# Two transformer blocks in one kernel: other buffers for two weight blocks, another order of slabs and steps

## The reference

```python
z = rmsnorm(x) @ w_in_2                       # qa ka va | qb kb vb | ga gb
qa, ka = rope(qa), rope(ka)                   # 4 heads of 2 components
ya = diff_attention(qa, ka, va, lam)          # softmax 0 minus lam * softmax 1, then a norm per head
yb = chunk_band_attention(qb, kb, vb, bias)   # 8 heads, relative bias, chunk mask
x = x + (sigmoid(ga) * (ya @ w_up_a) + sigmoid(gb) * (yb @ w_up_b)) @ w_out_2
x = x + cross_attention(rmsnorm(x), rmsnorm(mem), w_cq, w_ckv, w_co)
x = x + swiglu(rmsnorm(x))
return rmsnorm(x)
```

## Time and profile before

| | |
|---|---|
| median of 3 runs | 970.59 us (970.41 to 971.19) |
| the profiled execution | 972.24 us, span 970.3 us |
| TensorE (PE) busy | 924.0 us, 95% of the span, 4289 products |
| VectorE (DVE) busy | 629.2 us, 65% |
| ScalarE (ACT) busy | 458.1 us, 47% |
| GpSimd (POOL) busy | 30.6 us, 3% |
| DMA | 178.11 MB, 184 GB/s on average, above 330 GB/s in the first four of 40 slices |

### The profile page before, as it was taken

How to read it: one execution, slowest core, us unless ns; L and a number is a source line. 1 busy time by engine, 2 the same in 40 slices (tenths; PEclk the granted TensorE clock), 3 DMA queues, 4 the chain that set the end, 5 groups by cost and what they waited for, 6 DMA issues and landing times.

```text
span 970.3 us, 12075 instructions
## 1 busy us (share of the span) xinstructions
PE 924.0 (95%) x4289; PEld 741.7 (76%) x4289; DVE 629.2 (65%) x1016; ACT 458.1 (47%) x707; POOL 30.6 (3%) x42
## 2 busy tenths in 40 slices
PE   3989999999999999999999999999999999999997
PEld 3877655678788888887888777788788788888785
DVE  4887999988755555676766454578655555555544
ACT  0544422465544444544645443574545455555432
POOL 2110000010000000000000000000000000000000
PEclk9999999999999999999999999999999999999999
DMA  9999322766475665575655333245461465555531
GB/s 332 349 366 331 125 86 88 259 223 207 141 260 176 191 194 174 216 261 174 197 194 174 130 115 103 87 174 193 135 214 44 131 205 185 173 187 198 178 130 44
DMA packets 103031, 178.11 MB, mean 184 GB/s; under 512 B 6318, under 2 KB 52635, under 8 KB 102986
## 3 DMA queue, kind: packets, MB, share of 16 engines
q1 hardware_dynamic: 96138, 151.23, 47.4%
q0 software_dynamic: 6848, 26.28, 7.3%
HBM read 176.39 MB, written 1.05 MB: 183 GB/s over the span
## 4 chain that ended last, share of the span: by engine, by line
PE 73%; DVE 9%; issue 7%; ACT 2%; DMA 1%; POOL 0%; DVEq 0%; POOLq 0%; ACTq 0%
PE bank L553 18%; PE bank L555 18%; PE bank L554 18%; PE bank L959 10%; DVE conv_out L1883 4%; DVE w_lo L1664 1%; ACT w_hi L1208 1%; PE bank L938 1%; PE bank L632 1%; PE bank L784 1%; DMA ada_raw<-in_w_ada 1%; PE bank L1153 1%; PE bank L1169 1%; PE bank L800 1%; PE bank L1103 1%
## 5 line engine op out<-in xcount | busy, mean ns | idle before, releaser
L1664 DVE TENSOR_TENSOR w_lo<-raw_weights,w_hi 128x1024 fp32r<-128x1024 f32 x267 | 324.7, 1223 | 238.4 <-ACT w_hi L1208 236.9
L1208 ACT ACTIVATE w_hi<-raw_weights 128x1024 fp32r<-128x1024 f32 x267 | 281.1, 1058 | 304.8 <-PE bank L555 227.5
L553 PE MATMUL bank<-w_hi,a_hi 128*128 128x512 f32 x808 | 322.8, 399 | 5.9 <-DVE w_lo L1664 3.3
L555 PE MATMUL bank<-w_hi,a_lo 128*128 128x512 f32 x808 | 316.1, 391 | 0.0
L554 PE MATMUL bank<-w_lo,a_hi 128*128 128x512 f32 x808 | 315.6, 391 | 0.0
L553 PEld LDWEIGHTS bank<-w_hi,a_hi 128*128 128x128 f32 x808 | 152.2, 188 | 43.3 <-issue 7.3
L555 PEld LDWEIGHTS bank<-w_hi,a_lo 128*128 128x128 f32 x808 | 152.1, 188 | 32.4
L554 PEld LDWEIGHTS bank<-w_lo,a_hi 128*128 128x128 f32 x808 | 152.3, 188 | 29.8 <-issue 0.2
L959 PE MATMUL bank<-w_hi,ff_hi 128*128 128x512 f32 x176 | 55.2, 395 | 0.8 <-DVE hidden_rows L2161 0.5
L959 PE MATMUL bank<-w_hi,ff_lo 128*128 128x512 f32 x176 | 54.3, 389 | 0.0
L959 PE MATMUL bank<-w_lo,ff_hi 128*128 128x512 f32 x176 | 54.3, 390 | 0.0
(11 more groups left out here) (265 smaller groups left out, 870.4 us busy)
## 6 DMA issues: line engine op xcount, KB each, us to landing
raw_weights<-in_w_in SPq DMA_DIRECT2D x40, 1024.0 KB, 5.2
raw_weights<-in_w_ffn_in SPq DMA_DIRECT2D x44, 512.0 KB, 4.6
raw_weights<-in_w_gate_up SPq DMA_DIRECT2D x44, 512.0 KB, 4.6
ada_raw<-in_w_ada POOLq DMA_DIRECT2D x10, 1024.0 KB, 8.7
ada_start<-in_w_ada POOLq DMA_DIRECT2D x10, 1024.0 KB, 12.9
raw_weights<-in_w_ffn_out SPq DMA_DIRECT2D x9, 1024.0 KB, 5.0
raw_weights<-in_w_down SPq DMA_DIRECT2D x9, 1024.0 KB, 4.9
raw_weights<-in_w_out SPq DMA_DIRECT2D x8, 1024.0 KB, 5.2
```

Of the source, the lines that this page charges most:

```text
L553: pe.matmul(ps, hi[:, kt, ts], wh, start=start, stop=False)
L555: return pe.matmul(ps, lo[:, kt, ts], wh, start=False, stop=stop)
L1208: act.activation(w_hi[:, slot, 0:m], raw[:, b % RAW, half * PIECE:half * PIECE + m], ACT.Copy)\
L1664: dve.tensor_tensor(w_lo[:, slot, 0:m], raw[:, b % RAW, half * PIECE:half * PIECE + m], w_hi[:, slot, 0:m], ALU.subtract).then_inc(lo_read ...
```

## The change

- Ada block 10 gets the buffer `ada_start[4]` and waits for the first product of slab 4 only; block 11 gets a new buffer `ada_tail` over rows that were used up, and waits for the first four products.
- The second modulation columns come after one top-8 round instead of three. The second native gate piece comes ahead of the first step of the first attention instead of inside it.
- Second block: five plain slabs qb, kb, qa, ka, vb; va, the second memory keys, four gate slabs and half of the memory values are mixed. Rope works on 8 heads at a time. qb and kb are transposed in the third slab, qa in the fifth, ka in steps 1 and 2 of the banded attention; the second memory keys' transposes go behind the first query slab of the cross attention.
- Differential steps: a mixed piece at each step, ahead of its transposes; no products of constants. On VectorE the split comes ahead of the maximum, on ScalarE the eviction ahead of the exponential, in the banded steps as well.

```diff
-IN2_COLS = (E_QA, E_KA, E_QB, E_KB, E_VA, E_VB, E_GA, E_GA + W, E_GB, E_GB + W)
+IN2_COLS = (E_QB, E_KB, E_QA, E_KA, E_VB)
-MIXED = (("k", 1), ("a", 0), ("a", 1), ("b", 0), ("b", 1), ("v", 0))
-FILL2 = (1,) * 16 + (1, 0) * 4
-AHEAD2 = (0,) * 2 + (1,) * 13 + (0,) + (1, 0) * 3 + (1, 1)
+MIXED = (("h", E_VA), ("k", W), ("h", E_GA), ("h", E_GA + W), ("h", E_GB), ("h", E_GB + W), ("v", 0))
+FILL2 = (1,) * 24
+AHEAD2 = (0,) * 2 + (1,) * 22
+ROPE = (((0, 0), (0, 1)), ((0, 2), (1, 0)), ((1, 1), (1, 2)))
+TURN_AT = (1, 2)
+    ada_tail = sb("ada_tail", [P, BLK], at=u_at + 16384)
...
-        if 16 <= n < 20:
+        if n == 11:
+            return ada_tail[:]
+        if n == 10 or 16 <= n < 20:
             return ada_start[4 + n % 2][:]
...
-            if n >= 10:
+            if n == 10:
+                pool.wait_ge(ada_step, ada_count(4) + 1)
+            elif n == 11:
+                pool.wait_ge(ada_step, ada_count(4) + 4)
+                pool.wait_ge(sem["vec_turned"], 1)
+                pool.wait_ge(*ada_signal(9))
+            elif n >= 12:
                 pool.wait_ge(ada_step, ada_count(n // 2 - 1) + 4 * (n % 2 + 1))
...
             piece(P_IN1 + 24, U_IN1 + 6, 0, 4, pair=1, free=U_IN1 + 5)
             evicted(5)
+            piece(P_IN1 + 25, U_IN1 + 6, 1, 4, pair=1)
...
+        slab(P_IN2 + 4, U_IN2 + 1)
+        for j in range(3):
+            piece(P_IN2 + 8 + j, U_IN2 + 2, j, 4)
+            if j == 0:
+                for t in range(TT):
+                    pe.wait_ge(acc_free[t], U_IN2 + 2)
+                pe.wait_ge(sem["key_copied"], 2)
+                turn4(4, E_QB, z, sem["t2"])
+                turn4(6, E_KB, z, sem["t2"])
+        piece(P_IN2 + 11, U_IN2 + 2, 3, 4)
+        slab(P_IN2 + 12, U_IN2 + 3)
+        for j in range(3):
             piece(P_IN2 + 16 + j, U_IN2 + 4, j, 4)
             if j == 0:
                 pe.wait_ge(sem["t2_copied_act"], 2)
                 pe.wait_ge(sem["t2_copied_dve"], 2)
+                pe.wait_ge(sem["rope_sum"], TT)
+                turn4(6, E_QA, z, sem["t2"])
+        pe.wait_ge(sem["t2_copied_act"], 3)
...
         for n in range(len(DS)):
-            if n == 0:
-                hold(4, 6)
-            elif n % 2 == 0:
-                for _ in range(9):
-                    pe.matmul(bank[n // 6][:, 3 * P:4 * P], ident, ones, start=True, stop=True)
+            mixed_step(16 + n)
             d_turn(n)
             if n + 2 < len(DS):
                 d_scores(n + 2)
-            mixed_step(16 + n)
...
# ScalarE, project_slabs, behind conv(p + 4 * s + 4 + k)
+                    if s == 4 and k == 2:
+                        copy_pair(sem["t2"], 5, qaT[:, 0:2, :], 6, sem["t2_copied_act"])
# ScalarE, differential steps
+            mixed_out(16 + n)
             if n + 1 < 8:
                 d_exp(n + 1)
-            mixed_out(16 + n)
...
# VectorE, project_slabs, behind conv(p + 4 * s + 4 + k)
+                    if s in (3, 4) and k < 3:
+                        for i, op in ROPE[k]:
+                            rope(2 * (s - 3) + i, op)
+                    if s == 4 and k == 2:
+                        copy_pair(sem["t2"], 6, qaT[:, 2:4, :], 7, sem["t2_copied_dve"])
...
-                    top_rounds(0, range(0, 3), 2)
+                    top_rounds(0, range(0, 1), 2)
                     modulation_columns(1, 7)
+                    top_rounds(0, range(1, 3), 2)
...
             d_mix(n)
+            mixed_weights(16 + n)
             if n + 2 < 8:
                 d_max(n + 2)
-            mixed_weights(16 + n)
```

More of the change, by code:

```diff
@@ L453, in _ @@
             load(62 + j, slab_src(w2["w_ckv_2"], 4 * j, 0))
[L454 removed]
+        for s, c in enumerate(IN2_COLS):
             for j in range(2):
                 load(64 + 2 * s + j, slab_src(w2["w_in_2"], 4 * j, c))
[L457 removed]
         for m, (kind, c) in enumerate(MIXED):
             for j in range(2):
[L460 removed]
+                load(74 + 2 * m + j, slab_src(w2["w_in_2" if kind == "h" else "w_ckv_2"], 4 * j, c + D * (kind == "v")))
         for n, name in ((88, "w_up_b_2"), (90, "w_up_a_2")):
@@ L815, in gate_pieces @@
         def gate_pieces(n):
-            for j in range(max(filled(n), 1), filled(n + 1)):
+            for j in range(max(filled(n), 2), filled(n + 1)):
                 piece(P_IN1 + 24 + j, U_IN1 + 6 + j // 4, j % 4, 4, pair=1)
@@ L1034, in last_input_piece @@
             scores(1)
-            piece(P_IN2 + 23, U_IN2 + 5, 3, 4)
+            piece(P_IN2 + 19, U_IN2 + 4, 3, 4)
         def mixed_piece(j):
-            hi, lo = (mem_hi, mem_lo) if MIXED[j // 4][0] in "kv" else (a_hi, a_lo)
-            piece(P_IN2 + 24 + j, U_IN2 + 6 + j // 4, j % 4, 4, pair=1, hi=hi, lo=lo)
+            hi, lo = (a_hi, a_lo) if MIXED[j // 4][0] == "h" else (mem_hi, mem_lo)
+            piece(P_IN2 + 20 + j, U_IN2 + 5 + j // 4, j % 4, 4, pair=1, hi=hi, lo=lo,
+                  free=U_IN2 + 4 if j < 4 else None)
         def mixed_step(n):
@@ L1045, in mixed_step @@
                 mixed_piece(j)
[L1046 to L1051, removed]
+            if n in TURN_AT:
+                g = TURN_AT.index(n)
+                pe.wait_ge(sem["rope_sum"], 2 * TT)
+                pe.wait_ge(*((sem["t2_copied_act"], 4) if g else (sem["t2_copied_dve"], 3)))
                 for kk in range(2):
-                    kt = 2 * g + kk
+                    c = E_KA + (2 * g + kk) * P
                     for t in range(TT):
-                        last = pe.transpose(bank[7][:, kk * SEQ + t * P:kk * SEQ + (t + 1) * P],
-                                            k_rows[:, t, W + kt * P:W + (kt + 1) * P], ident)
-                last.then_inc(sem["key_turned"], 1)
+                        last = pe.transpose(bank[7][:, kk * SEQ + t * P:kk * SEQ + (t + 1) * P], z[:, t, c:c + P], ident)
+                last.then_inc(sem["t2"], 1)
         attention("b_", qbT, kbT, E_VB, 0, mixed_step, last_input_piece)
@@ L1127, in _ @@
         project(P_OUT2, U_OUT2, "m2_", True)
-        for s in range(2):
-            slab(P_CQ + 4 * s, U_CQ + s, 0, (N_CR) if s == 0 else None)
+        slab(P_CQ, U_CQ, 0, N_CR)
+        for t in range(TT):
+            pe.wait_ge(acc_free[t], U_IN2 + 7)
+        turn4(4, W, k_rows, sem["key_turned"])
+        slab(P_CQ + 4, U_CQ + 1)
         def value_piece(j):
@@ L1587, in _ @@
         conv(P_UB + 3)
-        mixed_slab_out(5)
+        mixed_slab_out(6)
         conv(P_UA, 2)
```

122 lines of the change are left out of this document (51 added, 71 removed).

## The result

The changed kernel takes 964.03 us (median of 6 runs, 962.5 to 966.78) against 971.7 for the kernel before beside it (6 runs, 970.41 to 976.15): a ratio of 0.9914, 95% interval 0.9897 to 0.9931. Forecast were 960.1 us with a range of 957.6 to 965.0, which is a ratio of 0.9892. So it is faster and inside the range: by 8.3 us by the ratio (7.7 by the two medians) where 10.5 were forecast. Taken off the 970.6 of the forecast the ratio gives 962.3, just outside the 958.8 to 962 that the prediction gave as the forecast's own range. The profiled execution took 963.36 us with a span of 961.6; that of before had 972.24 and 970.3.

A forecast was written before the change was run, and what follows sets the result against it. TensorE was taken to bound the kernel, VectorE from about 119 to 187 us. The terms -3.3 - 0.7 + 0 + 0.5 + 1.9 - 1.4 + 0.2 - 7.7 = -10.5 gave 960.1 us, range 957.6 to 965.

The forecast's parts named there:

- Ada blocks: Front end: blocks 10 and 11 land earlier, VectorE reaches the index weights sooner; -3.3 us, bounds -3.5 and +1.
- I charge 0.3 for it: Front end: 0.3 us charged for SyncE's weight load, pushed back by the ada blocks moved ahead of it.
- under 0.5: Sign to look for at the index weights: TensorE's wait there falls from 3.5 us to under 0.5.
- The queue rule: DMA engines alternate between busy queue rows packet by packet, so GpSimd's early block takes its gain from the weights' row.
- rival 2: Front end: blocks moved forward only change who is late, the 3.3 us are lost, 963.4 us; chance 0.12.
- Modulation columns: Ahead of two top-8 rounds: TensorE's wait of 1.2 us goes, only -0.7 reaches the end; bounds -1.2 and 0.
- Native piece: First attention: fills the 2.1 us wait, but some 2.6 come at the second exponential; 0, bounds -1.2 and +0.5.
- Order of the slabs: Second block: banded transposes wait +0.5, differential queries' copy +1.9, first mixed piece's wait gone -1.4, small/large product changes +0.2.
- "0" was right for them: Second keys' transposes moved behind the cross attention's first query slab, with two VectorE copies needed a slab later: 0.
- Differential steps: A piece at each of eight steps, no fillers: -7.7 us, bounds -8.5 and -3, including +1.2 at entry.
- rival 3: Fillers held TensorE's clock; mild, it falls at thin places, 961.8 to 963.5, chance 0.10; low throughout the differential stage, 989.
- rival 4: Better: the half-clock stretch at 777.06 doesn't come back, -1.7 us, 958.4 us; chance 0.07.

The follow-up runs named there:

- experiment 5: The kernel after with both ada blocks as before (block 10 in ada_raw behind four products, block 11 behind eight): 967.03 us, ratio 0.994.
- experiment 9: The kernel after with block 10 alone back in ada_raw behind four products, block 11 still in its own buffer: 967.61 us, ratio 0.9943.
- experiment 1: The kernel before without the products of constants in the differential steps, nothing in their place: 972.42 us, ratio 1.0009.
- experiment 3: The kernel after with ScalarE's copy of the differential queries one piece earlier and the fourth mixed slab's eviction ahead of the first differential exponential: 962.84 us, ratio 0.9914.
- experiment 6: The kernel after with the modulation columns behind three top-8 rounds again: 964.32 us, ratio 0.9909.
- experiment 4: The kernel after with the second native gate piece back inside the first step of the first attention: 963.15 us, ratio 0.9907.
- experiment 7: The kernel after with products of constants put into the waits ahead of its three half-rate stretches and at the differential entry: 961.0 us, ratio 0.9874.
- experiment 2: The kernel after with the products of constants back beside the mixed pieces in differential steps 0, 2, 4 and 6: 972.66 us, ratio 1.0005.
- experiment 10: The kernel after with both ScalarE moves and the constant products, but without the seven ahead of the first attention's first transposes: 961.1 us, ratio 0.9867.
- experiment 8: The kernel after with two ScalarE copies moved earlier and products of constants in the three waits left: 959.93 us, ratio 0.9864.

## Why the prediction was right, and where it was off

**Ada blocks (-3.3, came to -2.5).** The landing was as predicted: issued at 48.17, landed 9.7 later at 57.86, 0.33 of stall left where 0.7 was forecast. The mis-sized term is the displaced weight load, "I charge 0.3 for it": in the profiled execution it cost 1.62. That load was issued at 46.84 and took 12.8 us to land, against 8.4 for the same load before; TensorE's wait of 1.2 in place of "under 0.5" is its trace. Experiments 5 and 9 show that the blocks carry the part, mostly block 10 by one execution each, and that the forecast 3.3 comes where the front end starts a microsecond later. It is not the rule either: with a start 3 us later still, 1.6 is left. The prediction took the landing of one execution, 10.3 us, as given; it was 6.9 in experiment 1. The queue rule of the Trainium skill (DMA: Bandwidth & Descriptors, "Queues, rings and completion order") was weighed as leaning to rival 2. Its direction is what the trace shows, the weights' row paid 4.4 us of landing time for the block moved ahead of it (nothing in the three executions that started late); rival 2's conclusion isn't, since most of that landing time was slack. Rival 2's form as written, all 3.3 lost, fell.

**Modulation columns (-0.7).** The wait is gone, and from the gate sum to the last wait of the first attention the kernel after is 0.8 faster (129.91 against 130.70); with no half-rate stretch on either side it is 0.9 (129.77 in experiment 3), native piece included. The timed runs of experiment 6 can't tell it from nothing.

**Native piece (0).** 3.0 instead of the forecast 2.6 at the second exponential. Nothing came of it either way (experiment 4).

**Order of the slabs (+0.5, +1.9, -1.4, +0.2).** Measured waits were 0.8, 1.7, and none at the mixed piece. From 464 to the differential scores the kernel after gained nothing but lost 1.8, where +1.2 was forecast. Worked out: 1.3 of it is the half-rate stretch at 524.3 (experiment 7), and -0.9 are two sets of transposes of the second keys that left this stage; 1.8 - 1.3 + 0.9 = 1.4 stand beside the 1.2. Those transposes come back behind the first query slab as 0.8, so "0" was right for them in the end. The copy's wait hides a second limit just behind it (experiment 3).

**Differential steps (-7.7, came to -8.3).** 32.28 became 34.81 with four pieces more, 10.88: -8.35. The four steps between the pieces shown took 4.05 on average for the forecast 4.0, the entry wait was 1.09 for 1.2, and the wait at the last step fell to 0.2, by 0.9 instead of 0.7; the rest of the 0.6 more is not placed. Experiment 1 shows that the fillers weren't the prize, the covered place was; experiment 2 that TensorE bounds the loop.

**The clock (0 in the sum, came to +1.3).** This is the second place where the sum was off, and it was rival 3's mild form together with rival 4. The stretch at 777 was lost, -1.6 (from -7.1 to -8.7 in the last two rows of the table). Of the three new ones the first cost 0.1, the second 1.3 and the third 1.6: 1.3 + 1.6 - 1.6 = +1.3. The prediction named the wait ahead of the banded scores as a place for it. It named the differential entry too, where the clock held here, though it fell there in experiment 2 (596.3). It did not name the residual's transposes at 688, where it fell though nothing was changed there; the same work before, at 695, ran at full clock. Which of these places it falls in is luck, and so in part is the 1.3: this execution's mean clock is 0.993, the other five have 0.989 to 0.992. Rival 3's reason, that the fillers held the clock, has experiment 1 for it; its argument against, that dense work replaces them, held for the steps themselves.

One reading of the prediction is wrong, without weight for the sum: TensorE's waits over 60 ns add up to 39.3 us before, not some 30 (23.9 of them behind the first piece).

Sum of the rows: -2.5 - 0.8 + 0.1 + 1.8 - 8.3 - 0 + 2.6 - 1.6 = -8.7, the span's difference (2.6 is 0.8 of transposes, 1.6 of clock and 0.2 not placed).

## What to carry to other kernels

- Products that do no work and stand in a wait brought nothing when they were removed: part of the wait came back, and the clock was lower. Put real work in their place, then check that the stage is bound by that engine: adding the fillers back must cost their full length.
- A transfer moved ahead on a full DMA share is paid by the transfer it displaces. Price that one by its own slack, from its landing to the moment of its use, and expect price and gain to change from one execution to the next with the moment at which the front end starts (1.6 to 3.3 us here).
- Waits of one to three microseconds among small products can be followed by a stretch at half clock. Filling each with products of constants a little shorter than the wait took the ratio from 0.9914 to 0.9874 here; a stretch of 3.4 us cost 0.1 where VectorE bounds the stage, so there it hardly pays.

## What the runs showed of the hardware

- What a half-rate stretch costs depends on who bounds the stage. One of 3.41 us cost 1.3 to 1.6 us where TensorE is the bound, 0.1 in the first attention; one of 6.83 there cost 1.3 to 1.6 (131.12 to 131.37 against 129.8).
- Where it falls isn't fixed by the waits alone. The wait of 3.0 in the first attention was followed by none in experiments 2 and 3, by one in the kernel after and in experiment 10, by a double one in experiments 5 and 9. The transposes of a residual half, with a wait of 1.3 behind them, were followed by one at 777 before, at 688 after and at 771 in experiment 9. The shortest wait with one behind it was 1.1 us (experiment 2, at 596). With the waits filled none came in the profiled executions (experiments 7 and 8). What decides between equal places stays open.
- The first projection piece started at 39.7 to 43.6 us. Part of a late start is made up by the first gate sum: experiment 1 started 3.7 us behind the kernel before and stood 1.6 behind it there, with the same front end. So a span difference of a few us between two single executions of this kernel says nothing; compare from the first gate sum on.
